# Expert stage of a hybrid decoder step: where the last expert's scatters stand on the tensor engine

## The chip, the cores and the metric

The kernel runs on one core of a Trainium2 chip. The metric is the device time of one execution, in microseconds; before the change three runs took 1393.0, 1396.1 and 1396.65 us, median 1396.1. The engines are the tensor engine (PE, with its weight loads as PEld), VectorE (DVE), ScalarE (ACT), GpSimd (POOL) and SyncE (SP), which here issues the weight transfers. Each has its own instruction stream, and they wait for one another through semaphores.

## What is computed

The reference is one inference step of a decoder layer for 256 prompt tokens and 8 x 8 sample tokens, 320 in all: attention-like mixers (retention and mLSTM), an output projection, then a mixture of experts. The change is in the last part. Each token takes 4 of 32 experts; an expert multiplies its tokens by `w_up` (1024 x 2048), forms the clamped SwiGLU, and multiplies by `w_down` (1024 x 1024):

```python
def expert(args):
    xe, e = args
    hu = xe @ w_up[e] + b_up[e]
    gate = jnp.minimum(hu[:, :D_FF], SWIGLU_LIMIT)
    lin = jnp.clip(hu[:, D_FF:], -SWIGLU_LIMIT, SWIGLU_LIMIT)
    glu = gate * jax.nn.sigmoid(SWIGLU_ALPHA * gate)
    return ((lin + 1.0) * glu) @ w_down[e] + b_down[e]
...
out = jax.ops.segment_sum(y_sorted.astype(jnp.float32) * weights[:, None], tok, num_segments=T)
```

All weights are float32, 12 MB for an expert.

## The kernel before

The experts run one after the other in a loop of 32 passes. An expert's weights come in 12 pieces of 1 MB, 8 of `w_up` (piece c has 128 of its rows) and 4 of `w_down`, each with its own place in SBUF. SP issues them in that order, and issues a piece of the next expert as soon as PE has released the same piece of this one (`piece_done`), in the fixed order of the pieces. So a late release of one holds back all that follow.

An expert has as many slots as its count of tokens rounded up to 32, 64, 96 or 128. Every engine holds code for all four sizes and picks with `by_size` (lines 273 to 288), two compares and some jumps. The size of an expert shows in the trace in the width of DVE's first operation after the up products: 256, 512, 768 or 1024 elements for 32, 64, 96 or 128 slots. Counted from 0, expert 0 and 11 have 96, expert 17 has 128, experts 10, 12, 30 and 31 have 64, and 16 has 32.

One pass of PE (`expert`, lines 943 to 966) holds, in this order:

- `up`: the products with the 8 pieces (line 894) and the bias (line 898), into PSUM banks 0 to 3.
- `gather`: the next expert's tokens are picked out of the token rows by 72 products with a 0/1 matrix (line 865), into banks 4 and 5. There are two forms, for up to 64 slots and for more. ACT copies the result out (`xg_ready`).
- `scatter` 0 and 1: the previous expert's output `yd` is spread over the 256 prompt tokens by products with `G` (line 940), into banks 2, 3 and 4, 5. Two products each, shown as 4 records of a matmul. DVE adds each to the accumulator `acc` (line 1913).
- `turn_activations`: the activated values are transposed (line 904) when DVE has finished them (`act_ready`). They come from four DVE operations (lines 1894, 1895, 1898 and 1901), the last of which also needs ACT's sigmoid.
- three transposes of `Pg` (line 962), the scatter of the sample tokens (`scatter` 2, bank 3), and `down` (line 930), which releases the down pieces. Products of `down` with 64 slots take pieces in an order that needs the last piece from its second half on; those with 32 slots need all four at the start.

Then ACT copies the output (line 1263), and PE goes on with the next expert. After the last expert there are three more scatters, and DVE finishes (lines 1920 to 1937). The gather of that last pass picks nothing that is used; its form is chosen by column 32 of the counts, which holds the largest count.

DVE's pass: the 0/1 matrices for the next expert and for this one's scatter, the four operations, then the three additions.

Of the kernel before, what the change touches and what calls it, by code (L numbers as in the profile page):

```python
# [13 lines left out]
D = 1024  # L14
# [3 lines left out]
NT = 3  # L18
# [65 lines left out]
def build(nc, a):  # L84
# [6 lines left out]
    with ctx:  # L91
# [75 lines left out]
        counts = at(take(33), 33)  # L167
        counts_i = mem[:, cursor[0]:cursor[0] + 33].bitcast(I32)
        take(33)
# [188 lines left out]
        def _(sp):  # L358
# [60 lines left out]
            most = sp.value_load(counts_i[0:1, NE:NE + 1], min_val=0, max_val=NTOK)  # L419
# [13 lines left out]
        def _(pe):  # L433
# [456 lines left out]
            def up(it, slots):  # L890
                for c in range(UP):
                    pe.wait_ge(piece_in[c], 16 * (it + 1))
                    for out, cols, moving in up_products(slots, piece_slot(c, 2 * D)):
                        last = pe.matmul(out, xg[:, c, cols], moving, start=(c == 0), stop=False)  # L894
                    last.then_inc(piece_done[c], 1)
                pe.wait_ge(S("bsel_ready"), it + 1)
                for out, cols, moving in up_products(slots, bparts[:, 0:2 * D]):
                    last = pe.matmul(out, bsel[:, cols], moving, start=False, stop=True)  # L898
                last.then_inc(S("up_done"), 1)
# [36 lines left out]
            def scatter(it, t):  # L936

                for u in range(2):
                    out = psum[:, 2 + 2 * t + u, :] if t < 2 else psum[64 * u:64 * u + 64, 3, :]
                    last = pe.matmul(out, G[:, tok(t)], yd[:, u, :], start=True, stop=True)  # L940
                last.then_inc(S("scattered"), 1)

            def expert(r, e, it, count, count_next):
                ig = r * (NE + 1) + e
                pe.wait_ge(S("xg_ready"), ig + 1)
                pe.wait_ge(S("G_ready"), it + 1)
                pe.wait_ge(S("added"), 3 * it + 1)
                by_size(pe, count, lambda slots: up(it, slots))
                gather(ig + 1, count_next)

                pe.wait_ge(S("y_copied"), it + 1)
                pe.wait_ge(S("gate_ready"), it + 1)
                pe.wait_ge(S("lin_clipped"), it + 1)
                scatter(it, 0)
                pe.wait_ge(S("xg_ready"), ig + 2)
                scatter(it, 1)
                by_size(pe, count, lambda slots: turn_activations(it, slots))
                pe.wait_ge(S("Pg_ready"), it + 1)
                pe.wait_ge(S("added"), 3 * it + 2)
                for t in range(NT):  # L960
                    n = ROWS[t]
                    last = pe.transpose(psum[:, 2, tok(t)], Pg[0:n, t, :], ident[0:n, 0:n])
                last.then_inc(S("Pg_turned"), 1)
                scatter(it, 2)
                by_size(pe, count, lambda slots: down(it, slots))

            def last_scatter(its):
                pe.wait_ge(S("G_ready"), its + 1)
                pe.wait_ge(S("y_copied"), its + 1)
                pe.wait_ge(S("added"), 3 * its + 1)  # L970
                for t in range(NT):
                    if t == 2:
                        pe.wait_ge(S("added"), 3 * its + 2)
                    scatter(its, t)
# [7 lines left out]
            most = pe.value_load(counts_i[0:1, NE:NE + 1], min_val=0, max_val=NTOK)  # L982
            with pe.If(most > BIG_BLOCK):
                with pe.Fori(1, ROUNDS) as r:
                    gather(r * (NE + 1), None)
                    with pe.Fori(0, NE) as e:
                        expert(r, e, r * NE + e, None, None)
                last_scatter(NE * ROUNDS)
            with pe.Else():
                last_scatter(NE)  # L990
# [3 lines left out]
        def _(act):  # L994
# [281 lines left out]
            most = act.value_load(counts_i[0:1, NE:NE + 1], min_val=0, max_val=NTOK)  # L1276
# [24 lines left out]
        def _(pool):  # L1301
# [157 lines left out]
            most = pool.value_load(counts_i[0:1, NE:NE + 1], min_val=0, max_val=NTOK)  # L1459
# [13 lines left out]
        def _(dve):  # L1473
# [395 lines left out]
            def expert(r, e, it, count):  # L1869
# [33 lines left out]
                by_size(dve, count, lambda slots: weighted(128 if slots == 96 else slots))  # L1903
                by_size(dve, count, swiglu)
                add_scattered(it)

            def add_scattered(it):

                for t in range(NT):
                    dve.wait_ge(S("scattered"), 3 * it + t + 1)  # L1910
                    v = acc[:, t, :] if t < 2 else acc[:, 2, 0:512]
                    src = flat((2, 4, 3)[t], D if t < 2 else 512)
                    TT(v, v, src, ALU.add).then_inc(S("added"), 1)  # L1913
                dve.wait_ge(S("added"), 3 * it + 4)

            def finish(its):
# [9 lines left out]
                for t in range(NT):  # L1926
                    n = ROWS[t]
                    dve.wait_ge(S("scattered"), 3 * its + t + 1)
                    if t < 2:
                        TT(acc[:, t, :], flat(2 + 2 * t, D), gateF_p, ALU.mult).then_inc(S("added"), 1)  # L1930
# [13 lines left out]
            step(dve.reduce_max(counts[:, NE:NE + 1], counts[:, 0:NE], X))  # L1944
# [16 lines left out]
            most = dve.value_load(counts_i[0:1, NE:NE + 1], min_val=0, max_val=NTOK)  # L1961
# [46 lines left out]
```

## Time and profile before

| what | value |
| --- | --- |
| three runs | 1393.0, 1396.1, 1396.65 us |
| profiled execution | 1396.01 us |
| its span | 1394.2 us |
| PE matmuls busy | 1226.5 us, 88% |
| PE weight loads busy | 574.0 us, 41% |
| DVE busy | 385.1 us, 28% |
| ACT busy | 220.9 us, 16% |
| HBM read | 459.87 MB, 334 GB/s over the span |
| first up product | 413.1 us |
| an addition of DVE (line 1913), x96 | 1046 ns in the mean |
| a piece of `w_up`, from issue to landing, median | 25.2 us |
| a piece of `w_down`, the same | 18.2 us |

The profiled execution has its own time; durations below come from it. Times are from the start of the span. PE's busy time is an upper bound, since matmuls are pipelined and their ends are modelled. Shares are means over very different stages, so a stage is read by its own rows.

### The profile page before, as it was taken

How to read it: one execution, taken by the hardware profiler on the slowest of the kernel's cores; microseconds unless marked ns; L12 is line 12 of the kernel's file. 1: busy time of each engine (PE TensorE's matmuls, PEld its weight loads, DVE VectorE, ACT ScalarE, POOL GpSimd, SP SyncE). 2: the span in 40 equal slices, each digit the busy share in tenths (PEclk: the TensorE clock that was granted, in tenths of full speed). 3: DMA queues.
4: the chain of work that ended last, by engine and by line, in shares of the span. 5: the costliest groups of instructions: out<-in, count | busy, mean ns of one | idle time of the engine just before them, and what ended most of it. 6: DMA issues, size and time to landing. Idle time of an engine off the chain costs nothing.

```text
span 1394.2 us, 23096 instructions
## 1 busy us (share of the span) xinstructions
PE 1226.5 (88%) x8700; PEld 574.0 (41%) x8701; DVE 385.1 (28%) x845; ACT 220.9 (16%) x371; POOL 86.4 (6%) x168
## 2 busy tenths in 40 slices
PE   3799899778979999998899999799977898997895
PEld 2564545554453443443243343244422343342342
DVE  0125111555372211322222132112311122321126
ACT  0210323200130111211111121111111111111111
POOL 0102000236100000000000000000000000000002
PEclk9699999977989999999899999899998899998998
DMA  9966634525537999999999999999999999999993
GB/s 307 295 162 208 208 109 170 136 68 168 201 129 269 393 421 422 421 421 422 423 422 421 422 381 422 423 421 379 423 422 421 422 422 422 421 422 423 421 422 117
DMA packets 103754, 467.13 MB, mean 335 GB/s; under 512 B 10657, under 2 KB 30309, under 8 KB 54440
## 3 DMA queue, kind: packets, MB, share of 16 engines
q1 hardware_dynamic: 96530, 460.21, 83.6%
q10 hardware_dynamic: 6646, 5.33, 1.4%
q0 software_dynamic: 544, 1.12, 0.3%
q8 instruction: 25, 0.41, 0.1%
q14 instruction: 9, 0.07, 0.0%
HBM read 459.87 MB, written 6.16 MB: 334 GB/s over the span
## 4 chain that ended last, share of the span: by engine, by line
PE 58%; DMA 22%; SPq 10%; DVE 4%; issue 3%; POOL 2%; ACT 1%; ACTq 0%; POOLq 0%; PEldq 0%; DVEq 0%
DMA mem<-in_w_up 20%; PE psum L894 15%; PE psum L930 10%; SPq L399 9%; PE psum L940 7%; PE psum L577 6%; PE psum L865 4%; PE psum L562 3%; PE psum L581 2%; DMA mem<-in_w_mod 2%; PE psum L746 1%; PE psum L456 1%; PE psum L707 1%; PE psum L697 1%; PE psum L898 1%
## 5 line engine op out<-in xcount | busy, mean ns | idle before, releaser
L894 PE MATMUL psum<-mem 128*32 128x512 f32 (+2 forms) x2432 | 412.8, 637 | 77.7 <-DMA mem<-in_w_up 68.1
L894 PEld LDWEIGHTS psum<-mem 128*32 128x32 f32 (+2 forms) x2432 | 115.7, 123 | 363.1 <-issue 200.0
L930 PE MATMUL psum<-mem 128*32 128x512 f32 (+3 forms) x1024 | 211.5, 594 | 0.0
L1894 DVE TENSOR_SCALAR mem<-psum 128x256 f32<-128x256 f32 (+3 forms) x32 | 19.2, 601 | 589.1 <-PE psum L898 589.1
L940 PE MATMUL psum<-mem 128*128 128x512 f32 (+1 forms) x396 | 156.9, 607 | 1.7 <-ACT mem L1263 1.3
L1913 DVE TENSOR_TENSOR mem<-mem,psum 128x1024 f32<-128x1024 f32 (+1 forms) x96 | 100.4, 1046 | 101.1 <-PE psum L940 101.1
L930 PEld LDWEIGHTS psum<-mem 128*32 128x32 f32 (+3 forms) x1024 | 80.9, 127 | 103.3 <-issue 96.1
L865 PEld LDWEIGHTS psum<-mem 128*128 128x128 bf16 x2304 | 80.5, 99 | 23.6 <-issue 23.3
L577 PE MATMUL psum<-mem 128*128 128x512 f32 x192 | 87.2, 611 | 1.3 <-PE psum L456 1.3
L865 PE MATMUL psum<-mem 128*128 128x64 bf16 (+1 forms) x2304 | 84.5, 199 | 1.7 <-issue 1.7
L1240 ACT ACTIVATE mem<-mem 128x256 f32<-128x256 f32 (+3 forms) x32 | 17.9, 559 | 418.9 <-DVE mem L1894 418.9
L940 PEld LDWEIGHTS psum<-mem 128*128 128x128 f32 (+1 forms) x396 | 54.0, 172 | 53.2 <-issue 49.2
L1452 POOL CAST mem<-mem 128x128 bf16 (+1 forms) x33 | 10.6, 322 | 961.4 <-PE psum L930 961.4
L1263 ACT COPY mem<-psum 128x1024 f32<-128x1024 f32 x32 | 32.4, 1014 | 201.0 <-PE psum L930 201.0
L577 PEld LDWEIGHTS psum<-mem 128*128 128x128 f32 x192 | 37.0, 196 | 47.0 <-issue 47.0
L456 PE MATMUL psum<-mem 128*32 128x128 f32 x768 | 31.1, 327 | 24.1 <-DMA mem<-in_w_mod 20.2
L1010 ACT COPY mem<-psum 128x512 f32<-128x512 f32 (+10 forms) x79 | 29.9, 393 | 140.3 <-PE psum L577 80.1
L1240 ACT ACT_TABLE_LOAD x32 | 41.1, 1283 | 23.1 <-issue 23.1
L562 PE MATMUL psum<-mem 128*128 128x320 f32 x128 | 37.2, 452 | 5.1 <-DVE mem L1495 4.8
L456 PEld LDWEIGHTS psum<-mem 128*32 128x32 f32 x768 | 26.5, 133 | 28.6 <-DMA mem<-in_w_mod 17.0
L1866 DVE TENSOR_SCALAR mem<-mem 128x128 bf16<-128x128 f32 (+1 forms) x99 | 22.2, 281 | 40.2 <-issue 40.2
L562 PEld LDWEIGHTS psum<-mem 128*128 128x128 f32 x128 | 25.2, 199 | 16.5 <-DVE mem L1495 5.0
(258 smaller groups left out, 860.9 us busy)
## 6 DMA issues: line engine op xcount, KB each, us to landing
mem<-in_w_up SPq DMA_DIRECT2D x256, 1024.0 KB, 25.2
mem<-in_w_down SPq DMA_DIRECT2D x128, 1024.0 KB, 18.2
mem<-in_w_mod SPq DMA_DIRECT2D x12, 2048.0 KB, 15.1
mem<-in_w_in SPq DMA_DIRECT2D x8, 2048.0 KB, 13.7
mem<-in_w_out SPq DMA_DIRECT2D x2, 2048.0 KB, 20.0
mem<-in_state_ret SPq DMA_DIRECT2D x4, 512.0 KB, 6.3
mem<-in_state_mlstm_c SPq DMA_DIRECT2D x4, 512.0 KB, 7.2
out_ret_s<-mem SPq DMA_DIRECT2D x4, 512.0 KB, 3.2
```

The lines of the kernel that those rows point to most:

```text
L399: sp.dma_start(dst, src).then_inc(piece_in[c], 16)
L456: last = pe.matmul(psum[32 * t:32 * t + 32, q % BANKS, 0:128], cT[:, k, :], w[:, k, 128 * t:128 * t + 128], start=(k == 0), stop=(k == KD ...
L562: last = pe.matmul(psum[:, q % BANKS, 0:NTOK], w[:, k, 128 * m:128 * m + 128], hT[:, k, :], start=(k == 0), stop=(k == KD - 1))
L577: last = pe.matmul(psum[:, q % BANKS, :], hT[:, k, tok(t)], w[:, k, :], start=(k == 0), stop=(k == KD - 1))
L865: last = pe.matmul(psum[:, 4 + k // 4, 128 * (k % 4):128 * (k % 4) + slots], h2p[:, part, t, 128 * k:128 * k + 128], P[:, t, 0:slots], sta ...
L894: last = pe.matmul(out, xg[:, c, cols], moving, start=(c == 0), stop=False)
L930: last[c] = pe.matmul(psum[slots * q:slots * q + slots, 6 + u, :], turned, piece_slot(UP + c, 2, D)[:, piece % 2, 512 * u:512 * u + 512], ...
L940: last = pe.matmul(out, G[:, tok(t)], yd[:, u, :], start=True, stop=True)
L1010: act.copy(*pairs[-1]).then_inc(S("evacuated"), 1)
L1240: act.activation(sg.rearrange("p u n -> p (u n)")[:, 0:n], gt_.rearrange("p u n -> p (u n)")[:, 0:n], ACT.Sigmoid, scale=1.702).then_inc(S ...
L1263: act.copy(yd.rearrange("p u n -> p (u n)"), flat(6, D)).then_inc(S("y_copied"), 1)
L1913: TT(v, v, src, ALU.add).then_inc(S("added"), 1)
```

## The change

Four things change.

- `up` takes a range of pieces. PE runs the first two, then `scatter` 0 and 1, then the other six and the bias, then the gather, and goes from the gather directly to the turning. `up` is therefore entered by two switches on the size.
- The scatters write to banks 4, 5 and 6, 7, which nothing uses at that point, and no longer to 2, 3 and 4, 5.
- DVE adds scatters 0 and 1 ahead of its four operations, and scatter 2 behind them.
- Column 32 of the counts holds 0, and the largest count is in column 33, so that the gather of the last pass takes the form for up to 64 slots.

The `expert` of after begins at line 947, and all later lines of PE are numbered 2 to 4 higher.

PE's stream in the loop, from the gather to the turning, before. Line 865 is the gather in its two forms, 940 a scatter, 955 a wait, 279 and 280 the switch on size, 904 the turning for 32 slots:

```order
L865 MATMUL psum<-mem 128x64 x72
L872 UNCONDITIONAL_BRANCH
L861 REGISTER_ALU
L865 MATMUL psum<-mem 128x128 x72
L874 UNCONDITIONAL_BRANCH
L940 MATMUL psum<-mem 128x512 x2
L955 REGISTER_ALU
L940 MATMUL psum<-mem 128x512 x2
L279 COMPARE_AND_BRANCH
L280 COMPARE_AND_BRANCH
L904 MATMUL psum<-mem 128x128 x2
```

The same place after the change (908 is the turning):

```order
L865 MATMUL psum<-mem 128x64 x72
L872 UNCONDITIONAL_BRANCH
L861 REGISTER_ALU
L865 MATMUL psum<-mem 128x128 x72
L874 UNCONDITIONAL_BRANCH
L279 COMPARE_AND_BRANCH
L280 COMPARE_AND_BRANCH
L908 MATMUL psum<-mem 128x128 x2
```

The four products of the two scatters have left it. They now stand within the up products. This is PE's stream from the end of the first up part (896, the form for 128 slots) to the second one (the form for 32 slots, with its bias products at 902):

```order
L896 MATMUL psum<-mem 128x512 x8
L288 UNCONDITIONAL_BRANCH
L285 UNCONDITIONAL_BRANCH
L944 MATMUL psum<-mem 128x512 x4
L279 COMPARE_AND_BRANCH
L280 COMPARE_AND_BRANCH
L894 REGISTER_ALU
L896 MATMUL psum<-mem 32x512 x24
L902 MATMUL psum<-mem 32x512 x4
```

Before, all 32 up products of that form stood in one piece, ahead of the gather. On DVE, this is the end of the four operations and the additions (1913), before:

```order
L1901 TENSOR_TENSOR mem<-mem 128x1024
L288 UNCONDITIONAL_BRANCH
L285 UNCONDITIONAL_BRANCH
L1910 ISA
L1913 TENSOR_TENSOR mem<-mem,psum 128x1024
L1910 REGISTER_ALU
L1913 TENSOR_TENSOR mem<-mem,psum 128x1024
L1910 REGISTER_ALU
L1913 TENSOR_TENSOR mem<-mem,psum 128x512
```

And after, with the additions at 1917, up to the first of the four operations (1896) in the form for 32 slots:

```order
L1914 ISA
L1917 TENSOR_TENSOR mem<-mem,psum 128x1024
L1914 REGISTER_ALU
L1917 TENSOR_TENSOR mem<-mem,psum 128x1024
L279 COMPARE_AND_BRANCH
L280 COMPARE_AND_BRANCH
L1896 TENSOR_SCALAR mem<-psum 128x256
```

The two wide additions stand ahead of the switch that leads to the four operations; the narrow one has stayed behind them.

The diff, without the places that only read the largest count from its new column:

```diff
@@ -164,9 +164,9 @@
         gate = at(take(NT * 33), NT, 33)
         route = at_bf(take(NT * NE // 2), NT, NE)
         brout = at(take(NE), NE)
-        counts = at(take(33), 33)
-        counts_i = mem[:, cursor[0]:cursor[0] + 33].bitcast(I32)
-        take(33)
+        counts = at(take(NE + 2), NE + 2)
+        counts_i = mem[:, cursor[0]:cursor[0] + NE + 2].bitcast(I32)
+        take(NE + 2)
         hr = at(take(4), 4)
         mv2 = at(take(8), H, 2)
         top8 = at(take(24), NT, 8)
...
@@ -887,12 +887,16 @@
                             for lin in range(2) for q in range(2)]
                 return [(psum[:, b, :], slice(0, 128), weights[:, 512 * b:512 * b + 512]) for b in range(4)]
 
-            def up(it, slots):
-                for c in range(UP):
+            AHEAD = 2
+
+            def up(it, slots, pieces):
+                for c in pieces:
                     pe.wait_ge(piece_in[c], 16 * (it + 1))
                     for out, cols, moving in up_products(slots, piece_slot(c, 2 * D)):
                         last = pe.matmul(out, xg[:, c, cols], moving, start=(c == 0), stop=False)
                     last.then_inc(piece_done[c], 1)
+                if pieces[-1] < UP - 1:
+                    return
                 pe.wait_ge(S("bsel_ready"), it + 1)
                 for out, cols, moving in up_products(slots, bparts[:, 0:2 * D]):
                     last = pe.matmul(out, bsel[:, cols], moving, start=False, stop=True)
...
@@ -936,7 +940,7 @@
             def scatter(it, t):
 
                 for u in range(2):
-                    out = psum[:, 2 + 2 * t + u, :] if t < 2 else psum[64 * u:64 * u + 64, 3, :]
+                    out = psum[:, 4 + 2 * t + u, :] if t < 2 else psum[64 * u:64 * u + 64, 3, :]
                     last = pe.matmul(out, G[:, tok(t)], yd[:, u, :], start=True, stop=True)
                 last.then_inc(S("scattered"), 1)
 
...
@@ -945,32 +949,29 @@
                 pe.wait_ge(S("xg_ready"), ig + 1)
                 pe.wait_ge(S("G_ready"), it + 1)
                 pe.wait_ge(S("added"), 3 * it + 1)
-                by_size(pe, count, lambda slots: up(it, slots))
+                by_size(pe, count, lambda slots: up(it, slots, range(AHEAD)))
+                pe.wait_ge(S("y_copied"), it + 1)
+                scatter(it, 0)
+                scatter(it, 1)
+                by_size(pe, count, lambda slots: up(it, slots, range(AHEAD, UP)))
+                pe.wait_ge(S("added"), 3 * it + 2)
                 gather(ig + 1, count_next)
-
-                pe.wait_ge(S("y_copied"), it + 1)
-                pe.wait_ge(S("gate_ready"), it + 1)
-                pe.wait_ge(S("lin_clipped"), it + 1)
-                scatter(it, 0)
-                pe.wait_ge(S("xg_ready"), ig + 2)
-                scatter(it, 1)
                 by_size(pe, count, lambda slots: turn_activations(it, slots))
                 pe.wait_ge(S("Pg_ready"), it + 1)
-                pe.wait_ge(S("added"), 3 * it + 2)
                 for t in range(NT):
                     n = ROWS[t]
                     last = pe.transpose(psum[:, 2, tok(t)], Pg[0:n, t, :], ident[0:n, 0:n])
                 last.then_inc(S("Pg_turned"), 1)
                 scatter(it, 2)
+                pe.wait_ge(S("added"), 3 * it + 3)
                 by_size(pe, count, lambda slots: down(it, slots))
 
-            def last_scatter(its):
+            def last_scatter(its, gathers):
+                pe.wait_ge(S("xg_ready"), gathers)
                 pe.wait_ge(S("G_ready"), its + 1)
                 pe.wait_ge(S("y_copied"), its + 1)
                 pe.wait_ge(S("added"), 3 * its + 1)
                 for t in range(NT):
-                    if t == 2:
-                        pe.wait_ge(S("added"), 3 * its + 2)
                     scatter(its, t)
 
             gather_first()
...
@@ -1901,17 +1903,18 @@
                     TT(g_, l_, s_, ALU.mult).then_inc(S("act_ready"), 1)
 
                 by_size(dve, count, lambda slots: weighted(128 if slots == 96 else slots))
+                add_scattered(it, 0)
+                add_scattered(it, 1)
                 by_size(dve, count, swiglu)
-                add_scattered(it)
-
-            def add_scattered(it):
-
-                for t in range(NT):
-                    dve.wait_ge(S("scattered"), 3 * it + t + 1)
-                    v = acc[:, t, :] if t < 2 else acc[:, 2, 0:512]
-                    src = flat((2, 4, 3)[t], D if t < 2 else 512)
-                    TT(v, v, src, ALU.add).then_inc(S("added"), 1)
+                add_scattered(it, 2)
                 dve.wait_ge(S("added"), 3 * it + 4)
+
+            def add_scattered(it, t):
+
+                dve.wait_ge(S("scattered"), 3 * it + t + 1)
+                v = acc[:, t, :] if t < 2 else acc[:, 2, 0:512]
+                src = flat((4, 6, 3)[t], D if t < 2 else 512)
+                TT(v, v, src, ALU.add).then_inc(S("added"), 1)
 
             def finish(its):
 
...
@@ -1941,7 +1944,8 @@
             leave_rest(1, 1)
             leave_rest(2, 1)
             step(dve.tensor_copy(counts[:, 0:NE], psum[:, 0, 0:32]))
-            step(dve.reduce_max(counts[:, NE:NE + 1], counts[:, 0:NE], X))
+            dve.memset(counts[:, NE:NE + 1], 0.0)
+            step(dve.reduce_max(counts[:, NE + 1:NE + 2], counts[:, 0:NE], X))
             dve.tensor_copy(counts_i, counts).then_inc(S("counts_ready"), 1)
 
             dve.wait_ge(S("softmax_exp"), 1)
```

## Rows read from the trace of the kernel before

**Rows 1.** the DMA view, 460 to 1360 us: GB/s in 40 slices, then its queues.

```profile
GB/s 411 423 421 422 423 421 422 422 421 423 421 422 422 421 424 354 425 421 422 423 421 423 354 425 423 422 421 423 421 422 422 422 423 422 422 421 423 422 422 421
...
q1 hardware_dynamic: 51710, 376.58, 100.8%
```

**Rows 2.** busy time by window: length; PE, PEld, DVE, ACT, POOL; PEclk; DMA; GB/s.

```profile
440.00:460.00 20.00, 20.00 (x69) 7.96 (x71) 4.62 (x9) 2.32 (x4) 0.29 (x1) 1.00 0.49 165
...
899.00:907.00 8.00, 6.05 (x30) 0.90 (x31) 0.00 (x0) 0.00 (x0) 0.00 (x0) 0.57 1.01 422
...
1342.00:1358.00 16.00, 15.45 (x75) 6.07 (x72) 0.00 (x0) 2.30 (x2) 0.00 (x0) 1.00 1.02 423
```

**Rows 3.** timeline (start, length, instruction, idle before) of PE, then DVE, expert 0.

```profile
438.04 0.56 PE L865 MATMUL psum<-mem 128*128 128x64 bf16 x13 [1.66 <-issue]
438.55 3.68 PE L940 MATMUL psum<-mem 128*128 128x512 f32 x8
442.06 0.87 PE L904 MATMUL psum<-mem 128*128 128x128 f32 x6
...
437.44 0.96 DVE L1901 TENSOR_TENSOR mem<-mem 128x768 f32<-128x768 f32 x1
```

**Rows 4.** PE groups by shape over the expert stage, the 64-slot up products.

```profile
L894 PE MATMUL psum<-mem 128*64 128x512 f32 x768 | 174.0, 597 | 14.2 <-DMA mem<-in_w_up 11.3 <-issue 2.8
```

**Rows 5.** timeline of PE, expert 10: up, gather, turning.

```profile
707.26 4.97 PE L894 MATMUL psum<-mem 128*64 128x512 f32 x22 [0.38 <-issue]
...
725.44 4.30 PE L865 MATMUL psum<-mem 128*128 128x128 bf16 x72
...
733.07 0.63 PE L904 MATMUL psum<-mem 128*128 128x128 f32 x4
```

**Rows 6.** timeline of PE, then DVE, expert 11.

```profile
763.75 2.28 PE L865 MATMUL psum<-mem 128*128 128x64 bf16 x72
...
769.38 0.87 PE L904 MATMUL psum<-mem 128*128 128x128 f32 x6
...
766.71 0.96 DVE L1901 TENSOR_TENSOR mem<-mem 128x768 f32<-128x768 f32 x1
```

**Rows 7.** timeline of PE, then DVE, expert 12.

```profile
805.86 0.63 PE L904 MATMUL psum<-mem 128*128 128x128 f32 x4
...
802.39 0.69 DVE L1901 TENSOR_TENSOR mem<-mem 128x512 f32<-128x512 f32 x1
```

**Rows 8.** pieces of w_down issued about 891 us (expert 16's last): issue, landing.

```profile
L399 SPq MOVE mem<-in_w_down x1: 29/29/29, 891.3 to 891.3; - x1
...
DMA to landing us min/median/max: 21.5/22.4/23.4
```

**Rows 9.** timeline of PE, experts 16 and 17, then DVE, expert 17.

```profile
916.28 0.63 PE L930 MATMUL psum<-mem 128*32 128x512 f32 x3
...
955.79 1.11 PE L904 MATMUL psum<-mem 128*128 128x128 f32 x8
...
953.43 1.23 DVE L1901 TENSOR_TENSOR mem<-mem 128x1024 f32<-128x1024 f32 x1
```

**Rows 10.** timeline of PE and DVE, expert 31 and after.

```profile
1357.90 4.30 PE L865 MATMUL psum<-mem 128*128 128x128 bf16 x72
...
1360.06 0.69 DVE L1901 TENSOR_TENSOR mem<-mem 128x512 f32<-128x512 f32 x1
...
1365.53 0.63 PE L904 MATMUL psum<-mem 128*128 128x128 f32 x4
...
1367.86 7.03 PE L930 MATMUL psum<-mem 128*64 128x512 f32 x31
...
1378.22 1.23 DVE L1930 TENSOR_TENSOR mem<-psum,mem 128x1024 f32<-128x1024 f32 x1 [0.47 <-PE psum L940]
```

**Rows 11.** the last pieces of w_down: issue, then landing (the last is the longest).

```profile
L399 SPq DMA_DIRECT2D mem<-in_w_down x3: 333/333/333, 1343.2 to 1344.2; - x3
...
DMA to landing us min/median/max: 17.3/19.3/21.3
```

More of the change, by code:

```diff
@@ L418, in _ @@
             sp.wait_ge(S("counts_ready"), 1)
-            most = sp.value_load(counts_i[0:1, NE:NE + 1], min_val=0, max_val=NTOK)
+            most = sp.value_load(counts_i[0:1, NE + 1:NE + 2], min_val=0, max_val=NTOK)
             with sp.If(most > BIG_BLOCK):
@@ L981, in _ @@
                 expert(0, e, e, count, count_next)
-            most = pe.value_load(counts_i[0:1, NE:NE + 1], min_val=0, max_val=NTOK)
+            most = pe.value_load(counts_i[0:1, NE + 1:NE + 2], min_val=0, max_val=NTOK)
             with pe.If(most > BIG_BLOCK):
                 with pe.Fori(1, ROUNDS) as r:
+                    pe.wait_ge(S("xg_ready"), r * (NE + 1))
                     gather(r * (NE + 1), None)
@@ L987, in _ @@
                         expert(r, e, r * NE + e, None, None)
-                last_scatter(NE * ROUNDS)
+                last_scatter(NE * ROUNDS, (NE + 1) * ROUNDS)
             with pe.Else():
-                last_scatter(NE)
+                last_scatter(NE, NE + 1)
         @block.scalar
@@ L1275, in _ @@
                 expert(0, e, e, count, count_next)
-            most = act.value_load(counts_i[0:1, NE:NE + 1], min_val=0, max_val=NTOK)
+            most = act.value_load(counts_i[0:1, NE + 1:NE + 2], min_val=0, max_val=NTOK)
             with act.If(most > BIG_BLOCK):
@@ L1458, in _ @@
             pool.wait_ge(S("counts_ready"), 1)
-            most = pool.value_load(counts_i[0:1, NE:NE + 1], min_val=0, max_val=NTOK)
+            most = pool.value_load(counts_i[0:1, NE + 1:NE + 2], min_val=0, max_val=NTOK)
             with pool.If(most > BIG_BLOCK):
@@ L1929, in finish @@
                     if t < 2:
-                        TT(acc[:, t, :], flat(2 + 2 * t, D), gateF_p, ALU.mult).then_inc(S("added"), 1)
+                        TT(acc[:, t, :], flat(4 + 2 * t, D), gateF_p, ALU.mult).then_inc(S("added"), 1)
                         dve.wait_ge(S("added"), 3 * its + 2 + t)
@@ L1960, in _ @@
                 expert(0, e, e, count)
-            most = dve.value_load(counts_i[0:1, NE:NE + 1], min_val=0, max_val=NTOK)
+            most = dve.value_load(counts_i[0:1, NE + 1:NE + 2], min_val=0, max_val=NTOK)
             with dve.If(most > BIG_BLOCK):
```

## The prediction

> **What bounds the kernel now.** I read four views: the DMA's throughput over the expert stage, the tensor engine's (PE's) timeline where that throughput drops, the same around the last expert, and the landings of weight pieces.
>
> The throughput comes first [rows 1]. From 460 to 1360 us the queue of weight pieces keeps the 16 DMA engines full (100.8%), at 421 to 425 GB/s in 37 of 40 slices of 22.5 us. Two slices, at 797 to 820 and 955 to 977 us, show 354. A piece of 1024 KB at 422 GB/s takes 2.49 us, so the 12 pieces of an expert take 29.8 us. The stage is therefore a stream of weights, and a change on PE moves the end in three ways only: it makes a hole in the stream larger or smaller, it moves the stream's start, or it changes what is left after the last landing.
>
> Before 460 us the stream has its first hole: from 440 to 460 it moves 165 GB/s while PE is busy throughout [rows 2]. Expert 0 has 96 slots, and its down pieces come free only as PE works through them. The other two holes stand behind expert 12 (64 slots, after expert 11 with 96) and behind expert 17 (128 slots). At all three PE, not the DMA, sets when the next piece is asked for, so PE's time there counts in full.
>
> The tail: the last weight piece is issued at 1344.2 and lands 21.3 later, at 1365.5 [rows 11]. The last expert's up products end at 1357.9 and its down products run to 1367.86 + 7.03 = 1374.9 [rows 10]. So the tail is PE's chain, not the landing: gather, two scatters, turning, down.
>
> **The change part by part.** The count of matmuls is the same for every expert but the last. Two of three scatters (8 records) leave the place between gather and turning and go between the second and third up piece. From the start of the scatters to the start of the turning is 442.06 - 438.55 = 3.5 us [rows 3]. That is what an up stage gains and what the stretch behind it may lose.
>
> It does not lose all of it. Turning needs the activations, and VectorE (DVE) needs four operations for them after the up products. Before, the scatters covered these; now only the gather does. The turning then starts at the later of the end of the gather and the end of DVE's fourth operation. A switch on the expert's size now follows the gather directly; where an uncovered switch stands before products, PE waits 0.38 us for issue [rows 5]. I take 0.3 us for it where the gather ends last, and nothing where DVE does, since the wait covers it.
>
> Term 1, expert 0. DVE ends at 437.44 + 0.96 = 438.40, the gather at 438.55 [rows 3], so the whole 3.5 is regained; plus 0.3 for the switch. The added write of one zero in the counts stands ahead of the first up product and is one small DVE instruction, inside that 0.3. **+0.3**, bounds -0.2 and +1.7 (a second gap like the 1.66 us one in the gather, at its first pass [rows 3]).
>
> Term 2, the hole behind expert 12. Its PE chain starts in expert 10, which still waits for weights. Expert 10 (64 slots) has 725.44 - 707.26 = 18.2 us for its up stage [rows 5]. The products take 174.0 us for 12 such experts, 14.5 each [rows 4]; with 3.5 of scatters and some 0.5 of bias products that is 18.5, so +0.3. Its gather is the large one and ends at 725.44 + 4.30 = 729.7, the turning started at 733.07: 3.3 regained, 0.3 back for the switch. Expert 11 is then 2.7 early. Expert 11 (96): +3.5 in the up stage; DVE ends at 766.71 + 0.96 = 767.67 and the turning began at 769.38 [rows 6], so 1.7 regained: +1.8. Expert 12 (64): DVE ends at 803.08, the turning began at 805.86 [rows 7]: 2.8 regained, +0.7. Sum -2.7 + 1.8 + 0.7 = **-0.2**, bounds -2.7 (the later two at nothing, which would be the whole of this hole's gain) and +2.
>
> Term 3, the hole behind expert 17. Expert 16 (32 slots) needs all four down pieces for its first row of products; the last is issued at 891.3 and lands 23.4 later, at 914.7 [rows 8], and its down products began at 916.28 [rows 9]. So this expert gives 1.6, not 3.5: the landing is late next. Expert 17 (128): +3.5, and DVE ends at 953.43 + 1.23 = 954.66 against a turning at 955.79 [rows 9], so 1.1 regained: +2.4. Sum **+0.8**, bounds -1.6 and +2.5.
>
> Term 4, the tail. Expert 31 (64 slots). With no expert left, counts hold 0, the gather is of 64 slots, which takes 2.28 us in expert 11 [rows 6], where this one took 4.3. It would end at 1360.2, and DVE at 1360.06 + 0.69 = 1360.75. The turning began at 1365.53 [rows 10]: 4.8 gained. Against it: PE was busy 15.45 of 16 us in this expert's up stage [rows 2], takes 3.5 more there, and gets back only 2.8 by the earlier end of expert 30. With the same small loss in expert 30 I take +0.5. The down products would start near 1363.6 and want the last piece only in their second half, at 1367.1, after its landing at 1365.5. Behind them everything follows PE: ScalarE's copy, the last scatters, then DVE, which waits 0.47 for PE at 1378.22 [rows 10]. DVE's own work ahead of that hangs on the small third scatter, which moves too. **-4.3**, bounds -4.8 and -2.5.
>
> Cost at nothing: DVE's two additions (1.0 us in the mean) now stand before its four operations, but six more up pieces run meanwhile, which in experts of 32 slots are waited for at 2.49 us each. Up pieces 2 to 7 are released 3.5 us later, yet land some 25 us after their issue, so the queue covers it; where it is short (expert 12) a delay falls into the hole that PE makes anyway. The relaxed wait in the final scatter is hidden by DVE, busy from 1378.22 on.
>
> Sum: +0.3 - 0.2 + 0.8 - 4.3 = -3.4. The profiled run took 1396.0, 0.1 under the median: **1392.6 us**.
>
> A rule that speaks against the change: the Trainium skill, "Runtime: NRT & Kernel Launch", section on instruction fetch mechanics, says that a taken branch to a target outside the loaded code pages stops the engine for a fetch. The loop now has one switch more. The trace does not bear it out after the first pass: from 460 to 1360 only the queue of weights moved anything [rows 1]. It is the first rival below. Likewise "Advanced Engine Details and Errata", control flow timing, gives 108 ns for a compare and 51 ns for a jump; by it a switch of two of each would be an estimate of 0.3 us, and with it exposed in every term the sum would be some 0.9 nearer to zero. No row shows a branch alone.
>
> **Rivals.**
> A, slower: code loading. If the longer loop made PE load code in every pass, each expert whose PE time counts (0, 11, 12, 17, 31) would stall at both new switches by the 1.66 us seen once [rows 3]: 10 x 1.7 = +17, 1409. It decides from about 0.8 us per switch (7.6 / 10), where the sum passes +4.2. Against it stands [rows 1], where no code packets moved. Chance 0.04.
>
> B, slower or the same: the clock. PE waits for weights at new places (ahead of expert 16's down products, 1.8 us). Between 899 and 907 us the granted clock was 0.57, thus mostly 1.2 of 2.4 GHz, while PE waited for up pieces [rows 2]. If such a stretch fell on experts 0, 11, 12, 17 and 31 it would cost half its length, up to 3.4 us a time. Twice is +6.8: 1399.4. Against it: these experts have dense products. Once: 1396.0. Chance 0.07 for twice, 0.08 for once.
>
> C, no change: the tail's gain is eaten by terms 1 to 3 at their upper bounds (+6.2 in place of +0.9): 1397.9; halfway, 1395. Chance 0.20 for this stretch.
>
> D, faster: DVE's work does not delay the turning where I say (its fourth operation is shorter, or ends earlier relative to PE), terms 2 and 3 are -2.7 and -1: 1392.6 - 2.5 - 1.8 = 1388.3. Against it, the rows of DVE are of these very experts. Chance 0.14.
>
> E: the change does not do what it says: the last gather stays large. It would end at 1362.2, which regains 3.3 less 0.3 for the switch and 0.5 as before, so term 4 would be -2.5: 1394.4. The column read for the expert after the last is set to zero, so this has 0.03.
>
> My own case has 0.44, from 1390.5 to 1394.5. The range of 1389.5 to 1397.5 takes in C, E, B once, and part of D.
>
> A measurement of this kernel tells about 0.3%, 4.2 us, from no change; faster is then below 1391.9, which lies inside my case. The three allowances of 0.3 in terms 1 and 2 may each be nothing, which alone gives 1391.7, so I count half of my case as faster: with D 0.36. Slower, above 1400.3: A and half of B's double case, 0.08. Same: the rest, 0.56.
>
> **What would show it.** In the new profile the turning of expert 31 should begin some 4.3 us earlier, DVE-released and not gather-released; experts 11 and 17 should show PE idle 1.5 to 3 us before the turning, released by DVE; the last landing should be near 1366.4, 0.9 later by my first three terms; the two slices at 354 GB/s should remain. It would be wrong if PE shows idle time without releaser at the added switch, if the granted clock falls in dense experts, or if the holes vanish.

## The result: slower by 0.35%

The changed kernel took 1401.05 us in the median of 20 runs (1393.45 to 1409.71), the kernel before 1396.96 in 20 (1390.45 to 1406.63). The ratio is 1.0035, 95% interval 1.0018 to 1.0052, so 4.9 us slower, between 2.5 and 7.3; the two medians by themselves are 4.1 apart. In a second set, of 12 runs against 29, it was 1.0032 (1.0009 to 1.0055). The forecast was 1392.6, with a range that ended at 1397.5. One execution of the version with the scatters after piece 5 took 2072.75 us and is left out of its ratio below; its others took 1397.41 to 1407.51.

The profiled execution of the changed kernel seems to say the opposite: it took 1393.45 us, its span is 1391.6 against 1394.2. It was the fastest of the 20. The first up product shows why it can't be read by its total. This is PE's timeline at the start of expert 0, after the change, to be held against 413.1 us in the table of before:

```profile
407.66 5.36 PE L896 MATMUL psum<-mem 128*32 128x512 f32 x48 [3.72 <-DVE mem L1960]
412.95 3.71 PE L944 MATMUL psum<-mem 128*128 128x512 f32 x8
```

The stages ahead of the experts, which the change doesn't touch, were 5.4 us quicker. Over the ten further profiles of this study that start lies anywhere from 407.9 to 421.8. So I cut every profile into three: up to the first up product, expert 0 (up to the first up product of expert 1, it depends on the clock at its start), and the rest. For each run the table has these from its timeline and span; "tail" is from the landing of the last weight piece to the end. The ratio of each row is against runs of the kernel before that were taken together with it.

| kernel | first up product | expert 0 | rest | of it tail | measured ratio to before (95%) |
| --- | --- | --- | --- | --- | --- |
| before | 413.1 | 45.5 | 935.6 | 28.7 | |
| before, again | 416.6 | 48.4 | 935.3 | 28.7 | 1.0017 (0.9991 to 1.0044) |
| changed | 407.7 | 46.6 | 937.4 | 24.7 | 1.0035 (1.0018 to 1.0052) |
| changed, again | 414.0 | 47.1 | 938.1 | 24.7 | 1.0032 (1.0009 to 1.0055) |
| small gather alone | 411.9 | 50.1 | 932.4 | 26.7 | 1.0013 (0.9983 to 1.0042) |
| scatters after piece 5 | 413.2 | 49.6 | 940.0 | 27.0 | 1.0043 (1.0010 to 1.0076) |
| split scatters | 421.6 | 47.7 | 930.9 | 25.2 | 0.9995 (0.9963 to 1.0027) |
| split scatters, again | 418.6 | 48.0 | 930.6 | 25.2 | 0.9977 (0.9957 to 0.9997) |
| filled wait | 421.8 | 50.4 | 934.7 | 24.8 | 1.0028 (0.9996 to 1.0059) |
| longer DVE work | 415.9 | 51.0 | 947.7 | 26.2 | 1.0132 (1.0075 to 1.0188) |
| large last gather | 416.7 | 47.1 | 937.4 | 25.9 | 1.0041 (1.0016 to 1.0066) |
| second switch alone | 407.9 | 44.0 | 935.6 | 28.7 | 0.9988 (0.9957 to 1.0019) |

The rest repeats within 0.7 us for the same kernel, far better than whole runs. By it the change costs 2.3 us (937.4 and 938.1 against 935.6 and 935.3), though its tail is 4.0 shorter: the stream of weights ends 6.3 us later after expert 1's start (912.6 and 913.4 us against 906.9 and 906.6). Expert 0 adds some 1 us where its clock is alike (46.6 against 45.5). That makes 3.4 of the measured 4.9.

**The holes in the stream.** The DMA view of the changed kernel over the same 900 us, against [rows 1]:

```profile
GB/s 425 421 422 422 382 409 421 423 421 422 423 422 421 422 414 347 425 423 422 421 423 422 334 423 421 422 422 422 422 421 422 421 423 421 421 422 422 422 422 422
```

Two slices of before were low; now five are, in three places: 382 and 409 at 550 to 595 us, which had 423 and 421; 414 and 347 in place of 421 and 354; 334 in place of 354.

**The new one, behind expert 4.** The last down pieces of expert 5, issued as expert 4's down products release their places, in the changed kernel:

```profile
L399 SPq DMA_DIRECT2D mem<-in_w_down x3: 333/333/333, 568.3 to 572.2; - x3
...
DMA to landing us min/median/max: 4.8/4.9/6.7
```

and the four of the kernel before:

```profile
L399 SPq DMA_DIRECT2D mem<-in_w_down x4: 332/332/333, 569.1 to 573.6; - x4
...
DMA to landing us min/median/max: 6.3/7.7/10.2
```

No piece behind expert 1 landed sooner than 4.7 us after its issue in either kernel, so one that lands after 4.8 found an empty queue. With 6.3 at the least, before, they landed 2.49 apart, so there was always one in front. PE had run almost without waiting for a piece since expert 0 (0.57 us in all, in expert 2 of the kernel before), and the stream's reserve, the work still queued when a piece is issued, was nearly used up: by an estimate from 6.3 and 4.8 it was 1.5 us.

**PE in the large sizes.** Timeline of PE, changed kernel, experts 3, 11 (both 96 slots) and 17 (128), answering to [rows 6, 9]:

```profile
524.43 0.98 PE L908 MATMUL psum<-mem 128*128 128x128 f32 x6 [1.70 <-DVE mem L1903]
...
765.64 0.98 PE L908 MATMUL psum<-mem 128*128 128x128 f32 x6 [1.70 <-DVE mem L1903]
766.46 0.58 PE L963 MATMUL psum<-mem 128*128 128x128 f32 x3
766.98 1.57 PE L944 MATMUL psum<-mem 128*64 128x512 f32 x4
768.48 1.09 PE L918 MATMUL psum<-mem 128*96 128x512 bf16 x2
...
954.61 1.65 PE L908 MATMUL psum<-mem 128*128 128x128 f32 x8 [2.87 <-DVE mem L1903]
956.04 0.93 PE L963 MATMUL psum<-mem 128*128 128x128 f32 x3
956.91 1.89 PE L944 MATMUL psum<-mem 128*64 128x512 f32 x4
```

The waits for DVE are there as forecast, 1.7 and 2.9 us. Then comes what was not: the same four records of a scatter that took 1.08 us take 1.57 and 1.89. The windows right behind the waits of experts 11 and 17 (columns as in [rows 2], the granted clock is third from the end):

```profile
767.30:770.80 3.50, 3.50 (x8) 1.09 (x5) 0.97 (x3) 0.66 (x2) 0.00 (x0) 0.52 1.00 417
955.20:958.60 3.40, 3.40 (x13) 1.55 (x11) 0.00 (x0) 1.01 (x1) 0.00 (x0) 0.50 1.02 424
```

PE was at 1.2 GHz in two experts that had run at 2.4 throughout before. The second profile of the changed kernel has it at the same two places:

```profile
774.20:777.60 3.40, 3.40 (x8) 1.09 (x5) 0.69 (x2) 0.68 (x2) 0.00 (x0) 0.50 1.01 419
961.90:965.30 3.40, 3.40 (x15) 1.93 (x13) 0.00 (x0) 1.01 (x1) 0.00 (x0) 0.51 1.01 419
```

The end of down products lies 47.4 us after the previous expert's in expert 11 (43.6 before), 30.4 in expert 12 (29.2), 55.4 in expert 17 (52.3), 46.3 in expert 3 (44.1), in which the clock stayed at 1.00.

**A late release.** SP's own timeline, before and then after the change, for the up pieces of expert 19:

```profile
973.80 6.34 SPq L399 DMA_DIRECT2D mem<-in_w_up  x8
```

```profile
974.26 10.12 SPq L399 DMA_DIRECT2D mem<-in_w_up  x8
```

The eight issues now have the scatters between the second and the third. The third was issued at 979.8 and landed 6.9 later, 3.7 us after the one ahead of it where a full queue needs 2.49: a hole of 1.2 us, and of 1.7 in the second profile. The queue wasn't empty, though: the piece ahead landed at 983.0, 3.2 us after this issue. So what makes the landing late is not shown.

**The tail.** Timeline of the changed kernel, answering to [rows 10]:

```profile
1359.77 2.28 PE L865 MATMUL psum<-mem 128*128 128x64 bf16 x72
1361.93 0.69 DVE L1903 TENSOR_TENSOR mem<-mem 128x512 f32<-128x512 f32 x1
1362.68 0.74 PE L908 MATMUL psum<-mem 128*128 128x128 f32 x4 [0.63 <-DVE mem L1903]
...
1365.12 7.03 PE L934 MATMUL psum<-mem 128*64 128x512 f32 x31
...
1375.63 1.23 DVE L1933 TENSOR_TENSOR mem<-psum,mem 128x1024 f32<-128x1024 f32 x1 [0.64 <-PE psum L944]
```

The last piece, issued at 1343.1, lands 23.8 later, at 1366.9. Against the landing the turning begins 4.2 us before it; in the kernel before it began with it (1365.53, 1365.5).

### The profile page after: what moved, and what is told of

Its sections match the earlier page's. It is cut to its first block, busy times and chain, and to the rows that moved or that the text cites. A ratio compares the mean times of both kernels' runs of the same rounds, so it can differ in the third digit from the quotient of the medians.

```text
span 1391.6 us, 23211 instructions
## 1 busy us (share of the span) xinstructions
PE 1228.9 (88%) x8700; PEld 570.5 (41%) x8701; DVE 384.6 (28%) x846; ACT 218.5 (16%) x371; POOL 86.1 (6%) x168
## 4 chain that ended last, share of the span: by engine, by line
PE 63%; DMA 18%; DVE 7%; SPq 6%; issue 2%; POOL 2%; ACT 1%; ACTq 0%; POOLq 0%; PEldq 0%; DVEq 0%
PE psum L896 19%; PE psum L934 13%; DMA mem<-in_w_up 12%; PE psum L944 7%; PE psum L577 6%; SPq L399 5%; DMA mem<-in_w_down 5%; PE psum L562 3%; PE psum L865 2%; PE psum L581 2%; PE psum L746 2%; DMA mem<-in_w_mod 1%; PE psum L456 1%; PE psum L908 1%; PE psum L707 1%
## 5 line engine op out<-in xcount | busy, mean ns | idle before, releaser
L896 PE MATMUL psum<-mem 128*32 128x512 f32 (+2 forms) x2432 | 397.1, 612 | 45.7 <-DMA mem<-in_w_up 39.8
L934 PE MATMUL psum<-mem 128*32 128x512 f32 (+3 forms) x1024 | 226.8, 595 | 13.5 <-DMA mem<-in_w_down 13.5
L944 PE MATMUL psum<-mem 128*128 128x512 f32 (+1 forms) x396 | 159.9, 616 | 1.4 <-ACT mem L1265 1.4
L934 PEld LDWEIGHTS psum<-mem 128*32 128x32 f32 (+3 forms) x1024 | 84.0, 128 | 129.8 <-issue 94.5
L577 PEld LDWEIGHTS psum<-mem 128*128 128x128 f32 x192 | 35.9, 190 | 45.4 <-issue 45.4
L908 PE MATMUL psum<-mem 128*128 128x128 f32 x106 | 21.1, 315 | 14.9 <-DVE mem L1903 14.9
```

The source lines that it names most:

```text
L577: last = pe.matmul(psum[:, q % BANKS, :], hT[:, k, tok(t)], w[:, k, :], start=(k == 0), stop=(k == KD - 1))
L908: last = pe.transpose(flat(0, D)[:, 128 * j:128 * j + 128], gt_.rearrange("p u (w i h) -> p u w h i", w=2, h=2)[:, j // 4, j // 2 % 2, j % ...
L934: last[c] = pe.matmul(psum[slots * q:slots * q + slots, 6 + u, :], turned, piece_slot(UP + c, 2, D)[:, piece % 2, 512 * u:512 * u + 512], ...
```

## The experiments

Theory P: what counts is PE's time in runs of experts in which it paces the stream, and it grew by the uncovered wait for DVE. Theory L: the late release of up pieces 2 to 7 makes the holes. Theory C: PE's clock falls behind the new waits.

**Small gather alone.** The kernel before with the counts' column of zero:

```diff
+            dve.memset(counts[:, NE:NE + 1], 0.0)
-            step(dve.reduce_max(counts[:, NE:NE + 1], counts[:, 0:NE], X))
+            step(dve.reduce_max(counts[:, NE + 1:NE + 2], counts[:, 0:NE], X))
```

> The kernel before with one part of the change alone: the gather of the last pass takes the form for up to 64 slots. All theories: the last gather takes 2.2 us in place of 4.3 and the two scatters behind it cover DVE, so the tail from the last landing (1365.5 in the kernel before) to the end gets 2.1 us shorter, 26.6 in place of 28.7, and the expert stage is otherwise that of before: holes behind experts 12 and 18 pieces as before (6.1 us of excess over 2.49 us per piece from expert 2 on), total 2.1 us faster than before. If the tail were bound by DVE's finishing work, it would be unchanged.

The tail is 26.7, 2.0 us shorter where 2.1 were expected. Experts 11, 12 and 17 last what they did (43.5, 29.2, 52.3). The rest is 932.4, 3 us less and 1 more than I can account for. The measured ratio can't tell 2 us.

**Scatters after piece 5.**

```diff
-            AHEAD = 2
+            AHEAD = 6
```

> The changed kernel with the scatters between the sixth and seventh up piece in place of the second and third. Theory L (late release): up pieces 2 to 5 are released 3.6 us earlier, so the delays at pieces 2 and 3 of experts 13 and 19 (0.9 and 1.2 us of excess) vanish, while the holes at the down pieces of experts 5, 13 and 18 stay (2.1, 3.2, 4.3 us): 1.2 to 2 us faster than the changed kernel. Theory P (only PE's time per dense expert counts): the excess from expert 2 on stays at 11.9 us but moves to the down pieces, no change of the total. Theory C (where PE waits decides the clock): experts of 32 slots wait in longer stretches for their last pieces, more half-clock time, and the total is up by 1 us or more.

Theory L was right on one point: the holes at piece 2 of expert 19 and at pieces 2 and 3 of expert 13 are gone. But the whole is worse (940.0). The tail loses 2.3 of its gain, since the scatters now stand just ahead of the last up products, when there is little landing left to hide them. Expert 10 takes 34.4 us in place of 32.1 for the same reason. And expert 3 takes 48.0, with a half-clock stretch of 3.4 us behind its wait, so that the hole at expert 5's pieces is 4.5 us in place of 2.0. The stream ends no sooner than in the changed kernel (913.0 us after expert 1's start). So the holes of the late release were not what made the change slower.

This run also bears on theory C. The same waits, of experts 3, 11 and 17:

```profile
532.99 0.98 PE L908 MATMUL psum<-mem 128*128 128x128 f32 x6 [1.70 <-DVE mem L1903]
...
778.18 0.98 PE L908 MATMUL psum<-mem 128*128 128x128 f32 x6 [1.70 <-DVE mem L1903]
...
966.04 1.22 PE L908 MATMUL psum<-mem 128*128 128x128 f32 x8 [2.87 <-DVE mem L1903]
```

and the windows behind them:

```profile
534.80:538.20 3.40, 3.40 (x8) 1.09 (x5) 1.02 (x3) 0.50 (x2) 0.00 (x0) 0.50 1.02 424
778.20:785.00 6.80, 6.80 (x25) 3.21 (x26) 2.21 (x7) 1.30 (x3) 0.23 (x1) 1.00 1.01 420
966.00:973.00 7.00, 6.96 (x27) 3.62 (x28) 2.17 (x7) 1.44 (x2) 0.16 (x1) 1.00 1.02 424
```

The clock fell in expert 3, and in experts 11 and 17 it did not (45.8 and 54.5 us in place of 47.4 and 55.4). So such a wait is not always followed by a half-clock stretch.

**Split scatters.** Scatter 1 back between gather and turning:

```diff
-                scatter(it, 1)
                 by_size(pe, count, lambda slots: up(it, slots, range(AHEAD, UP)))
                 pe.wait_ge(S("added"), 3 * it + 2)
                 gather(ig + 1, count_next)
+                scatter(it, 1)
...
-                add_scattered(it, 1)
                 by_size(dve, count, swiglu)
+                add_scattered(it, 1)
```

> The changed kernel with scatter 1 back between gather and turning, scatter 0 staying between the second and third up piece. Theory P (the wait for DVE that the scatters used to cover): the turning of the experts with 96 slots no longer waits 1.7 us, that of 128 waits 1.1 in place of 2.9, that of 64 not at all; each dense expert takes 1.3 (64) to 1.8 us (96, 128) less, expert 4 ends some 3 us sooner and the hole at expert 5's down pieces (2.1 us) closes, those at 13 and 18 shrink by 2 to 3 in all; the tail gets 1.2 us longer. Total 3 to 4 us faster than the changed kernel. Theory L (late release of pieces 2 to 7): half of the delay is gone, holes at the down pieces stay; 0.5 us faster and 1.2 slower in the tail, no gain.

> The version with scatter 1 between gather and turning, once more. If its expert stage is really shorter, the stretch from the landing of expert 1's last piece to the end is again near 926 us (925.8 before), 4 us under the kernel before and 6 under the changed one, and the median is 0.1 to 0.3% under the kernel before. If the first profile was luck in the half-clock stretches, it is back near 930.

The rest is 930.9 and 930.6: 7.0 us under the changed kernel (mean of its two profiles) and 4.7 under the one before. Expert 11 takes 44.1, expert 12 29.6, expert 17 52.8. PE in expert 11 of the second profile:

```profile
771.98 2.28 PE L865 MATMUL psum<-mem 128*128 128x64 bf16 x72
774.10 1.97 PE L944 MATMUL psum<-mem 128*128 128x512 f32 x4
775.96 0.98 PE L908 MATMUL psum<-mem 128*128 128x128 f32 x6
776.78 0.58 PE L963 MATMUL psum<-mem 128*128 128x128 f32 x3
777.29 1.08 PE L944 MATMUL psum<-mem 128*64 128x512 f32 x4
```

There is no idle time ahead of the turning, and the last scatter takes 1.08 us again. The gain is twice what theory P alone predicted: the half-clock stretches are gone too (theory C), and so is the hole at expert 19, 1.2 and 1.7 us (theory L). At expert 5's pieces 1.1 and 0.7 us are still lost. Measured in one set with the changed kernel, the medians are 1393.05 and 1402.53; against the kernel before it is level in one set and 0.2% faster in the other. It keeps 3.5 us of the tail.

**Filled wait.** The changed kernel, with products that nobody reads in place of the idle time:

```diff
+                if slots >= 96:
+                    pe.wait_ge(S("added"), 3 * it + 3)
+                    for u in range(slots // 32 - 1):
+                        pe.matmul(psum[:, 6 + u % 2, :], G[:, 0:128], yd[:, u % 2, :], start=True, stop=True)
                 pe.wait_ge(S("act_ready"), it + 1)
```

> The changed kernel with extra products whose result nobody reads, in the two large sizes only, in the time in which PE waits for DVE before the turning: 2 of 0.86 us for 96 slots, 3 for 128. Theory C (the clock): the half-clock stretches right behind these waits (3.4 us at 767 in expert 11, 3.4 us at 955 in expert 17) vanish, which gives back 1.7 us each, so holes 13 and 18 shrink by 1.5 us each, total 3 us faster than the changed kernel. Theory P: PE's time is the same, the half-clock stretches come from elsewhere; no change, or up to 0.3 us slower.

PE starts the turning no sooner by this, and yet expert 11 takes 45.9 in place of 47.4, expert 17 53.9 in place of 55.4, the rest 934.7 in place of 937.7. The windows over the same work:

```profile
770.00:790.00 20.00, 19.90 (x199) 8.72 (x192) 5.95 (x11) 2.74 (x5) 0.00 (x0) 1.00 1.01 421
955.00:975.00 20.00, 19.81 (x126) 10.18 (x125) 5.49 (x5) 2.98 (x4) 0.00 (x0) 1.00 1.01 422
```

The clock stays at full speed, and the holes at experts 13 and 18 are 1.6 us smaller each. So a half-clock stretch costs about 1.5 us, 3 in all. By itself this one profile doesn't show that the idle time is the cause, since with the scatters after piece 5 the clock held in these two experts with the idle time in place. All twelve profiles together do bear it out: in experts 3, 11 and 17, of 15 idle times of 1.70 us or more 10 were followed by a half-clock stretch; where there was no more than 1.07 us, none of 21 experts had one. In whole runs the difference (1.0028 against 1.0035) is too small to be seen.

**Longer DVE work.** One of DVE's four operations done twice:

```diff
+                    TSC(l_, lin_in, 7.0, -7.0, ALU.min, ALU.max).then_inc(S("clipped_once"), 1)
+                    dve.wait_ge(S("clipped_once"), it + 1)
                     TSC(l_, lin_in, 7.0, -7.0, ALU.min, ALU.max).then_inc(S("lin_clipped"), 1)
```

> The changed kernel with DVE's second operation done twice in every expert (same result). Theory P (PE waits for DVE before the turning, and that wait counts wherever PE paces the stream): experts of 96 slots take 1.0 us more, of 64 some 0.8, of 128 1.3, of 32 up to 0.4; the time from the first up product to the end grows by 5 to 8 us against the changed kernel (984.0 and 985.2). Theory L (only the late release of up pieces counts): no change there.

The rest grows by 10.0 us, 1.5 of it in the tail, the run by 1% (4 runs). From the first up product to the end it is 14.1 us more where 5 to 8 were expected, but 4 of these are in expert 0, whose clock was at half for 9 us here and not at all in the changed kernel. PE in experts 3 and 11:

```profile
538.23 1.55 PE L908 MATMUL psum<-mem 128*128 128x128 f32 x6 [2.69 <-DVE mem L1905]
539.58 0.93 PE L963 MATMUL psum<-mem 128*128 128x128 f32 x3
540.44 1.97 PE L944 MATMUL psum<-mem 128*64 128x512 f32 x4
...
784.00 1.55 PE L908 MATMUL psum<-mem 128*128 128x128 f32 x6 [2.69 <-DVE mem L1905]
```

```profile
537.60:544.40 6.80, 6.17 (x17) 3.14 (x18) 1.26 (x2) 1.30 (x3) 0.00 (x0) 0.50 1.01 420
783.30:790.00 6.70, 6.00 (x17) 3.00 (x18) 1.34 (x2) 1.30 (x3) 0.00 (x0) 0.50 1.02 423
```

The wait is 1.0 longer, but expert 3 takes 50.1 in place of 46.3: the half-clock stretch, absent there in the changed kernel, is now there and 6.8 us long. That is part of why I had expected too little. Theory L had this at no change, so the late release alone doesn't explain what PE's order costs.

**Large last gather.** The column holds 65, for the large form.

```diff
-            dve.memset(counts[:, NE:NE + 1], 0.0)
+            dve.memset(counts[:, NE:NE + 1], 65.0)
```

> The changed kernel with the last pass's gather in its form for more than 64 slots, as before the change. Gather ends 1.4 us later than DVE's fourth operation, so the tail (24.7 us from the last landing) becomes 26.2 and the rest is that of the changed kernel: 1.5 us slower. If the gather's form were of no effect because DVE is late, the tail stays 24.7.

The tail is 25.9, 1.2 longer. 1.5 were expected. So of the 4.0 gained in it, 1.2 is the gather's form once the scatters have moved, and 2.8 the place of the scatters with the large gather; in the old order the form alone gave 2.0. The rest as a whole is not longer (937.4): the hole at expert 19 did not open in this execution, so that one is not in every execution of the changed order.

**Second switch alone.** The kernel before, with `up` in two parts and nothing between:

```diff
-                by_size(pe, count, lambda slots: up(it, slots))
+                by_size(pe, count, lambda slots: up(it, slots, range(AHEAD)))
+                by_size(pe, count, lambda slots: up(it, slots, range(AHEAD, UP)))
```

> The kernel before with the up products entered by two switches on size, after piece 2 too, and nothing between them. The switch is covered by queued products (my forecast took 0.3 us for it): experts 11, 12 and 17 take 43.6 to 43.9, 29.2 to 29.5 and 52.3 to 52.6 us, total +0 to 1. If the second switch is what makes the dense experts of the changed kernel 1.2 us longer, expert 12 takes 30 or more and the total rises by 3.

Experts 11, 12 and 17 take 43.6, 29.2 and 52.1, the rest is 935.6: this switch costs nothing. The switch that now follows the gather directly is another. Where the gather ends last, in expert 10 of the changed kernel, it leaves no idle time either:

```profile
723.02 4.30 PE L865 MATMUL psum<-mem 128*128 128x128 bf16 x72
727.16 0.69 PE L908 MATMUL psum<-mem 128*128 128x128 f32 x4
```

**Both kernels again.**

> The kernel before, once more, for a second profile. If the stages ahead of the experts set the spread between executions, the first up product moves by several us (413.1 in the first profile) while the time from the landing of expert 1's last piece to the end stays at 929.7 within 1 us. If the spread came from the expert stage, that stretch would move too.

> The changed kernel, once more. Its first profile had an early first up product (407.7) and was the fastest of 20 executions. If the stages ahead of the experts make that, the second profile starts the experts near 413 to 421 and takes 931.5 within 2 us from the landing of expert 1's last piece to the end (half-clock stretches behind the waits for DVE may or may not fall there), against 929.7 in the kernel before. Median near 1401, 0.3% above the kernel before.

Both came out as expected. The front part moved (413.1 and 416.6, 407.7 and 414.0), the rest did not (935.6 and 935.3, 937.4 and 938.1).

## Why the prediction was wrong

**The tail, term 4: right.** -4.3 forecast, -4.0 measured, with DVE releasing the turning, PE 0.5 later against the landings, and the rest of the chain behind PE. The last landing at 1366.9, where 1366.4 was forecast, is luck: this execution reached the experts 5.4 us earlier, and from there to the last landing it took 6.8 us more where 0.9 were forecast.

**The step that failed: "a change on PE moves the end in three ways only", with the holes taken as the three that the trace showed.** I priced PE's time where a hole was, and not where the stream's reserve was small. Experts 1 to 4 run on PE almost without waiting for a piece too. The changed kernel takes 3.5 us more from the landing of expert 1's last piece to the end of expert 4 (+0.5, -0.4, +2.2 and +1.2 by experts), 3.9 in the second pair of profiles, more than the reserve of some 1.5: expert 5's pieces lost 2.1 us against 2.49 us a piece, 2.8 in the second profile. The reserve isn't a sharp line: the split version is 1.5 us later there and loses 1.1 and 0.7. This term stood nowhere in the sum.

**Terms 2 and 3 had the mechanism and the wrong size.** Term 2 was -0.2. The gain in expert 10 was there (3.4), but expert 11 cost +3.8 for the +1.8 forecast and expert 12 +1.2 for +0.7, together +1.6. Some 1.5 of that is the half-clock stretch. The other 0.5 per expert are small hand-overs: the scatters take 3.63 from start to start inside the up products where 3.5 was taken, and some 0.1 goes at each seam. Term 3 was +0.8 and came out at +1.2 (0.5 in the second pair, as the kernel before lost more there), with +3.1 in expert 17 for +2.4, half of which is the half-clock stretch: with the wait filled it was +1.6. Rival B had the fall of the clock, though behind waits for weights, and set against it that "these experts have dense products". The change itself had put idle time of 1.7 and 2.9 us into them, which the forecast itself works out in terms 2 and 3.

**"Up pieces 2 to 7 are released 3.5 us later, yet land some 25 us after their issue, so the queue covers it; where it is short (expert 12) a delay falls into the hole that PE makes anyway" failed as well.** At expert 13 the queue didn't cover it either (0.8 and 0.7 us lost), but there the delay did fall into the hole that PE makes anyway. At expert 19, whose queue is still short after the hole at expert 18, it did not: 1.2 and 1.7 us. A hole there stands in three of the five profiles in which these pieces were issued so late, and in none of the seven with an earlier issue.

Term 1: +0.3 forecast, +1.1 measured (46.6 against 45.5). The gap of 1.66 us inside the first gather is not in the changed kernel's profile, so its gather ended early and PE waited 1.70 us for DVE there too. The 3.5 regained hung on that gap: with the second switch alone there was none, and expert 0 took 44.0 us in the old order.

**The switches.** Rival A, code loading, is out: from 460 to 1360 us only the queue of weights moved anything in the changed kernel too, and experts 11, 12 and 17 have no such stall. The 0.3 us that terms 1 and 2 allow for an uncovered switch is not seen either, at the second switch or behind the gather of expert 10. By "Advanced Engine Details and Errata" of the Trainium skill, control flow timing, a switch was an estimate of 0.3 us; no trace here shows a branch alone, and nothing of it shows on PE at these two places.

The sum as measured, each hole named by the expert whose pieces are late: expert 0 +1.1, the new hole +2.1 or 2.8, hole 13 +1.6, hole 18 +1.2 or 0.5, hole 19 +1.2 or 1.7, tail -4.0; +3.2 by the first pair of profiles and +3.7 by the second, against 4.9 (2.5 to 7.3) in whole runs. What stays open: why expert 3 (and expert 0), with the same idle time of 1.70 us as expert 11, kept its full clock in all three profiles with the changed order, while with the scatters after piece 5 expert 3 lost it and experts 11 and 17 kept it. Late release was not tested without moving the scatters' cover too; its share rests on the landings alone.

## What to carry to other kernels

Where a transfer stream bounds a stage, look for how much reserve the slower experts leave it, not only for the holes it already has: work that is added where the reserve is thin opens a new one. Before moving work out of a place, ask which engine's latency it was covering there; with half of it left in place the part behind expert 0 was 4.7 us shorter than before, with all of it moved 2.3 longer. And where whole runs scatter by 1%, cut the profiles at a mark that the change can't reach; the part behind it here repeated within 0.7 us.

## What the hardware showed

An idle time of 1.70 us on PE in an otherwise dense expert was followed by 3.4 us at half the clock (expert 11, in all three profiles of it with the changed order), one of 2.87 us likewise (expert 17), and one of 2.69 us by 6.8 and 6.7 us (experts 3 and 11 with the longer DVE work). It is not so each time: 1.70 us in expert 3 was followed by none in the same three profiles, and with the scatters after piece 5 neither 1.70 us in expert 11 nor 2.87 us in expert 17 was. In all, 10 of 15 such idle times in experts 3, 11 and 17 had a stretch behind them, and none of 21 with at most 1.07 us had. Idle times of 0.63 us (experts 12 and 31) were followed by none. With the first two filled with products that nobody reads, the part behind expert 0 was 3.0 us shorter, in one profile.

The pieces of 1 MB issued into an empty queue at experts 5 and 13 of the changed kernel landed 4.7 to 4.9 us later; in a full queue they landed 2.49 us apart.

The stages ahead of the experts, the same in all these kernels but for the counts' columns, ended anywhere between 407.7 and 421.8 us, and expert 0 took 44.0 to 51.0.
